# Delta rule stage: output gate blocks of the last token group moved into the four last steps, normalised rows reloaded in parts, the next stage's weights given other places

## The reference

```python
h = _rmsnorm(x, norm_w)
u = (h @ w_in).astype(f32)
gla_u, rwkv_u = u[..., :GLA_IN], u[..., GLA_IN:]
...
gla_out = o.reshape(B, T, GLA_VW) * jax.nn.silu(gg)
...
rg = rwkv_u[..., RWKV_SHIFT_W:]                      # output gate, the "z" blocks
mixed = shifted_cols + (prev - shifted_cols) * rwkv_mu
r, rk, rv, wl, al = _split(mixed, RWKV_SHIFT_SPLITS)
...
S = S * w_t + sa (kk_t a_t) + v_t k_t ;  y_t = S r_t   # per head, token after token
...
rwkv_out = (y + bonus) * jax.nn.silu(rg)
return x + jnp.concatenate([gla_out, rwkv_out], axis=-1) @ w_out
```

## Time and profile before

| | us |
|---|---|
| median of the runs (3) | 3676.9 |
| lowest and highest run | 3675.92, 3686.67 |
| span of the profiled execution | 3670.3 |

### The profile page before, as it was taken

How to read it: one execution, slowest core, us unless ns; L and a number is a source line. 1 busy time by engine, 2 the same in 40 slices (tenths; PEclk the granted TensorE clock), 3 DMA queues, 4 the chain that set the end, 5 groups by cost and what they waited for, 6 DMA issues and landing times. The chain is left out here.

```text
span 3670.3 us, 83152 instructions
## 1 busy us (share of the span) xinstructions
PE 3499.6 (95%) x34784; PEld 2817.1 (77%) x34784; DVE 2059.5 (56%) x4664; ACT 1718.7 (47%) x3161; POOL 1347.3 (37%) x1681
## 2 busy tenths in 40 slices
PE   8999998899899999999998989999999997999999
PEld 7878786688787877888786877777777776788777
DVE  4566766755655656555555436666666665344422
ACT  3455555522555556555553344444444442444522
POOL 5433331232445554545543323232232220544332
PEclk9999999999999999999998999999999998999999
DMA  4322211232110111101112341111111113322322
GB/s 136 90 66 81 61 53 35 81 104 93 30 41 24 41 30 30 41 24 41 30 33 89 129 144 48 43 43 39 46 38 43 43 37 111 82 74 70 104 81 92
DMA packets 252243, 231.26 MB, mean 63 GB/s; under 512 B 9120, under 2 KB 223072, under 8 KB 251872
## 3 DMA queue, kind: packets, MB, share of 16 engines
q1 hardware_dynamic: 251872, 225.94, 20.3%
HBM read 192.35 MB, written 33.55 MB: 62 GB/s over the span
## 5 line engine op out<-in xcount | busy, mean ns | idle before, releaser
L195 PE MATMUL bank<-hT_cut,arena_cut 128*128 128x512 f32 x2048 | 803.8, 393 | 0.0
L188 ACT ACTIVATE arena<-bank 128x512 f32<-128x512 f32 (+1 forms) x584 | 315.7, 569 | 578.4 <-PE bank L196 294.4
L194 PE MATMUL bank<-hT_cut,arena_cut 128*128 128x512 f32 x1240 | 553.9, 447 | 0.0
L196 PE MATMUL bank<-hT_cut,arena_cut 128*128 128x512 f32 x1240 | 488.6, 394 | 0.0
L194 PE MATMUL bank<-arena_cut,hT_cut 128*128 128x512 f32 (+1 forms) x1280 | 459.4, 359 | 28.5 <-DVE arena_cut L1148 23.9
L188 ACT ACTIVATE arena<-arena 128x512 f32<-128x512 f32 (+3 forms) x674 | 350.0, 555 | 251.9 <-POOL arena L1596 191.7
L195 PE MATMUL bank<-arena_cut,hT_cut 128*128 128x512 f32 (+1 forms) x1280 | 448.0, 350 | 0.0
L195 PEld LDWEIGHTS bank<-hT_cut,arena_cut 128*128 128x128 f32 x2048 | 387.4, 189 | 78.3 <-issue 18.3
L189 ACT ACTIVATE arena<-arena 128x256 f32<-128x256 f32 (+2 forms) x336 | 210.3, 627 | 417.2 <-DVE arena L178 192.7
L2846 POOL TENSOR_TENSOR arena_cut<-arena,arena_cut 128x256 fp32r<-128x256 f32 x272 | 218.1, 831 | 409.2 <-ACT arena_cut L188 409.1
L711 POOL TENSOR_TENSOR arena_cut<-arena,arena_cut 128x256 fp32r<-128x256 f32 x288 | 216.3, 778 | 410.8 <-ACT arena_cut L188 410.8
(11 more groups left out here) (269 smaller groups left out, 7192.2 us busy)
## 6 DMA issues: line engine op xcount, KB each, us to landing
arena<-in_w_in SPq DMA_DIRECT2D x100, 512.0 KB, 3.8
arena<-in_attn_w_in SPq DMA_DIRECT2D x144, 256.0 KB, 2.8
arena<-in_rec_w_in SPq DMA_DIRECT2D x62, 512.0 KB, 4.1
x_after<-arena SPq DMA_DIRECT2D x32, 512.0 KB, 2.6
arena<-x_after SPq DMA_DIRECT2D x32, 512.0 KB, 4.2
arena<-in_x SPq DMA_DIRECT2D x16, 512.0 KB, 3.6
h_after<-hT SPq DMA_DIRECT2D x4, 2048.0 KB, 7.7
hT<-h_after SPq DMA_DIRECT2D x4, 2048.0 KB, 16.8
```

Of the source, the lines that this page charges most:

```text
L188: return e.activation(out, a, f, bias=bias, scale=scale)
L194: pe.matmul(out, a[0], b[0], start=start, stop=False)
L195: pe.matmul(out, a[0], b[1], start=False, stop=False)
L196: return pe.matmul(out, a[1], b[0], start=False, stop=stop)
```

## The change

In `delta_rule`:
- The four z blocks of the last group (units 12 to 15) leave `front` and become a stream `gate(u)` of their own, one for each of steps 32 to 35, eight ticks each over the ten rounds. The odd steps of the last group have 11 ticks in place of 17, and `steps_in` and `bonus` come one and two ticks after the end of v.
- In the gate stream, at the end of each of those steps, ACT does `tanh`, DVE makes (tanh + 1) * z in `tz`, and `late(u)` multiplies it into `oT`. `carry` of the last group writes its output alone. Unit 15's `late` is the last operation of the stage on DVE.
- The hi part of group 3 is put into the columns of group 1 in place of group 0, and its rounding waits chunk by chunk for group 2's last z block.
- SP loads the columns of group 0 after the load of block v of unit 12, groups 1 and 3 after the last z block (now in step 35), and group 2 in `gla`, behind unit 1.
- Eight tiles of `front` are laid where `gla`'s value weights will be, and the three weight buffers stand first in both stages, so that `load_v(0)` waits for the last front instead of the last z block, and `load(0)` for the z block before the last. On SP's list both still stand behind the loads of groups 1 and 3.

In `gla`: the hi part of group 0 goes to the columns of group 2 of `hT`; ACT rounds group 0 as soon as its columns are loaded, ahead of `settle`, but behind `wide_split(0)`; group 2 is awaited by `lows(2)` and by its rounding.

```diff
-def gla(k):
-    freed = k.freed
+def gla(k, h_saved):
+    freed, ready, moved = k.freed, k.ready, k.moved
...
+    w_at = [k.room_cut(2 * KC * P) for _ in range(3)]
     wide = k.room_cut(4 * KC * P)
-    w_at = [k.room_cut(2 * KC * P) for _ in range(3)]
...
-    hi_of = lambda g, c: k.hT_cut[:, c, cols_of(g // 2 if g == 2 else 0)] if g else k.oT_cut[:, c // 2, T // 2 + c % 2 * G:T // 2 + (c % 2 + 1) * G]
+    hi_of = lambda g, c: k.hT_cut[:, c, cols_of((2, 0, 1, 0)[g])]
...
-        for done in freed:
+        for done in freed[0]:
             sp.wait_ge(*done)
         load_v(0)
+        for done in freed[1]:
+            sp.wait_ge(*done)
         load(0)
         k.settle(sp)
...
+            if u == 1:
+                sp.wait_ge(*Fpe.by("z1", 1))
+                sp.wait_ge(*moved[2])
+                sp.dma_start(k.hT[:, :, cols_of(2)], h_saved[:, :, cols_of(2)]).then_inc(*h_got.did("in"))
...
         wide_split(0)
+        for done in ready:
+            a.wait_ge(*done)
+        run(cut(0))
         split(0)
         k.settle(a)
-        run(cut(0))
         low_kept(0)
...
@@ in delta_rule @@
-    hi_of = lambda g, c: k.hT_cut[:, c, cols_of(g // 2 if g == 2 else 0)] if g else ...
+    hi_of = lambda g, c: k.hT_cut[:, c, cols_of(g // 2)] if g else ...
...
+              for p, kind in [(None, "w")] + [(p, kind) for p in range(4) for kind in ("krv" if g == LAST else "krvz")]]
+    blocks += [("z", LAST, p) for p in range(4)]
...
-            ahead, ticks, went = stream(front, 0), 17 + (8 if i % 8 == 0 else 0), 0
+            ahead, went = stream(front, 0) if i < SN else gate(UN - 4 + i - SN), 0
+            ticks = 8 if i >= SN else 11 if i >= SN - 8 and i % 2 else 17 + (8 if i % 8 == 0 else 0)
...
+            if n == index["v", LAST, 0]:
+                sp.wait_ge(*Zpe.by("z", 7))
+                load_h(0)
-        sp.wait_ge(*Fpe.by("z", UN - 1))
-        for g in range(NG):
-            sp.wait_ge(*moved[g])
-            sp.dma_start(k.hT[:, :, cols_of(g)], h_saved[:, :, cols_of(g)]).then_inc(*h_got[g].did("in"))
+        sp.wait_ge(*Zpe.by("z", UN - 1))
+        load_h(1)
+        load_h(3)
...
@@ on_pe, front @@
                 squares()
                 yield from block("v", g, p, Fpe)
-                yield from block("z", g, p, Fpe, {2: bonus})
-                yield
+                if g == LAST:
+                    yield
+                    yield
+                    bonus()
+                else:
+                    yield from block("z", g, p, Zpe, {2: bonus})
+                yield
+
+        def gate(u):
+            yield from block("z", *groups[u], Zpe)
...
@@ on_act @@
+        def gated(u):
+            a.wait_ge(*Zpe.by("z", u))
+            if u > UN - 4:
+                a.wait_ge(*Zm.by("m", u - UN + 3))
+            elif u:
+                a.wait_ge(*Zv.by("z", u - 1))
+            k.tanh(tz, fb.at("z", u), scale=0.5).then_inc(*Za.did("th"))
...
@@ on_dve, front @@
+                if g == LAST:
+                    yield
+                    steps_in()
+                    yield
+                    bonus()
...
+        def gate(u):
+            yield from block()
+            v.wait_ge(*Za.by("th", u))
+            stt(v, tz, tz, 1.0, fb.at("z", u), ALU.add, ALU.mult).then_inc(*Zv.did("z"))
+            if u < UN - 1:
+                late(u)
+
+        def late(u):
+            g, p = groups[u]
+            out = k.oT[:, 4 + p, cols_of(g)]
+            v.wait_ge(*Zv.by("z", u))
+            v.wait_ge(*Cv.by("out", 2 * u + 1))
+            v.tensor_tensor(out, out, tz, ALU.mult).then_inc(*Zm.did("m"))
...
+            if g == LAST:
+                ts(v, k.oT[:, 4 + p, tok], y_at, 0.5, ALU.mult).then_inc(*Cv.did("out"))
...
-        in_turn(nothing, solve, scores, carry, front)
+        in_turn(nothing, solve, scores, carry, front, gate)
+        late(UN - 1)
...
-    k.freed = [Fpe.by("z", UN - 1)]
+    k.freed = [[Fpe.by("bn", UN - 1), Fa.by("v2", UN - 1), Fv.by("bn", UN - 1), Fp.by("bk", UN - 1)], [Zpe.by("z", UN - 2)]]
+    k.ready = [h_got[0].by("in")]
+    k.moved = moved
```

More of the change, by code:

```diff
@@ L2325, in gla @@
     on_dve()
[L2326 to L2327 removed]
+    k.freed = [(3 + c, Fpe.by("v1", UN - 1)) for c in range(2)] + [
+        ((BN - 4 + i) % 3, Fpe.by(kinds[i], UN - 1)) for i in (1, 2, 3)]
     k.ready = [Fpe.by("z1", UN - 1), Bv.by("out1", 1)]
@@ L2351, in delta_rule @@
     w_lo, w_hi = ([x[1].rearrange("p (s c n) -> p s c n", s=2, c=KC)[:, s] for x in w_at] for s in range(2))
+    kf, r_at, gl, av, kat, b_at, sq, kk_at = (room(G) for _ in range(8))
     wa, up, cols = room(G), room(512), room(80)
@@ L2362, in delta_rule @@
     sh = room(G + 1)
-    kf, r_at, gl, av, kat, tz = (room(G) for _ in range(6))
+    tz = room(G)
     vf_at = rooms(2, G)
-    b_at, sq, kk_at, rk_at, tt, eb, en = (room(G) for _ in range(7))
+    rk_at, tt, eb, en = (room(G) for _ in range(4))
     ar_at, beta, kappa, bon_at = rooms(2, 2 * G), room(G), room(G), rooms(3, G)
@@ L2430, in taken, with in_turn @@
         return s.by(name, n)
-    def in_turn(cut, solve, scores, carry, front):
+    def in_turn(cut, solve, scores, carry, front, gate):
         rounds = 10
@@ L2789, in front @@
                 turn = p == 3 and g + 1 < NG
-                yield from block("z", g, p, {c: (lambda c=c: round_h(g + 1, c)) for c in range(KC)} if turn else {})
-                a.wait_ge(*Fpe.by("z", u))
-                k.tanh(tz, fb.at("z", u), scale=0.5).then_inc(*Fa.did("z"))
-                yield
+                if g == LAST:
+                    yield
+                    yield
+                else:
+                    yield from block("z", g, p, {c: (lambda c=c: round_h(g + 1, c)) for c in range(KC)} if turn else {})
+                    gated(u)
+                yield
+        def gated(u):
[6 more added lines that the diff above has]
+        def gate(u):
+            yield from block("z", *groups[u])
+            gated(u)
         def scores(s):
@@ L2881, in front, with gate @@
                 yield from block("v", g, p, {5: removal})
-                yield from block("z", g, p)
+                if g == LAST:
+                    yield
+                    yield
+                else:
+                    yield from block("z", g, p)
                 yield
+        def gate(u):
+            yield from block("z", *groups[u])
         split(0)
         k.settle(pool)
-        in_turn(nothing, nothing, nothing, nothing, front)
+        in_turn(nothing, nothing, nothing, nothing, front, gate)
     def on_dve():
@@ L2976, in front, with gate @@
                 mixed("v", vf_at[u % 2])
-                yield from block({1: steps_in, 5: bonus}, g + 1 if p == 3 and g + 1 < NG else None)
-                v.wait_ge(*Fa.by("z", u))
-                stt(v, k.oT[:, 4 + p, cols_of(g)], tz, 1.0, fb.at("z", u), ALU.add, ALU.mult).then_inc(*Fv.did("z"))
-                yield
+                if g == LAST:
+                    yield
+                    steps_in()
+                    yield
+                    bonus()
+                else:
+                    yield from block({1: steps_in, 5: bonus}, g + 1 if p == 3 and g + 1 < NG else None)
+                    v.wait_ge(*Za.by("th", u))
+                    stt(v, k.oT[:, 4 + p, cols_of(g)], tz, 1.0, fb.at("z", u), ALU.add, ALU.mult).then_inc(*Zv.did("z"))
+                yield
+        def gate(u):
+            yield from block()
+            v.wait_ge(*Za.by("th", u))
+            stt(v, tz, tz, 1.0, fb.at("z", u), ALU.add, ALU.mult).then_inc(*Zv.did("z"))
[7 more added lines that the diff above has]
+            v.tensor_tensor(out, out, tz, ALU.mult).then_inc(*Zm.did("m"))
         def halve(l, s, ring, steps, t1, vec):
```

34 lines of the change are left out of this document (23 added, 11 removed).

## The result

The changed kernel is slower: 3710.84 us (median of 4 runs, 3707.28 to 3714.4) against 3677.61 us for the kernel before in the same comparison. The ratio is 1.0084, 95% interval 1.0073 to 1.0096, so 27 to 35 us. The direction was the forecast one, the size was not: +33 in place of +14.5, above the range.

The account below looks back on a forecast made before the run. PE was taken as without gap while fronts run, with 22.7 us idle in steps 32 to 35. Terms -9.2 + 11.1 + 11.1 + 1.5 = +14.5 us on 3676.9 gave 3691 us, range 3671 to 3703.

Parts of the forecast that it names:

- Odd steps: The last group's four odd steps: 25.7 us each in place of 28.0, transposes waiting for DVE's `ka`; -9.2 us.
- Even steps: Steps 26, 28 and 30, between the last group's odd steps: no term in the sum, so 0.
- Late steps: Steps 32 to 35, to the stage's end: z chunks, the gate's chain and table loads cost +11.1 us net.
- the rival with PE at 1.2 GHz in the late steps: In steps 32 to 35 z costs twice its time in two of them: +12 more, 3703 us; chance 0.12.
- Loads: Groups 1 and 3 land late, first value products come 25.4 us after the last z product; net +11.1 us.
- a head start of DVE's rests: At GLA's start the value products run beside DVE's rests, now further ahead: 2.0 us given back.
- Small ones: Loads of group 0 beside unit 12 and group 2 in `gla` stall PE: +1.5 us; other changes nothing.
- PE stays the bound: Rival for the last group's odd steps: -22 in place of -9.2, sum +1.7, 3679 us; chance 0.20.
- the whole of z hidden: Rival: steps 32 to 35 take in all of z, -6.6, with odd steps -22; sum -16, 3661 us; chance 0.12.
- loads at the end cost nothing: Rival at the next stage's start: `settle` is met before the stage ends; sum +3.4, 3680 us; chance 0.08.

Follow-up runs that it names:

- v early: The changed kernel with 17 ticks kept in the last group's odd steps, z's ticks left empty: 3697.3 us, ratio to the kernel before 1.0049.
- the tanh table: The changed kernel with a one-column tanh added at the end of odd steps 25, 27 and 29: 3706.7 us, ratio to the kernel before 1.0071.
- the clock: The changed kernel with the last group's bonus product multiplied five times in place of once: 3705.3 us, ratio to the kernel before 1.0071.
- gate deferred: The changed kernel with DVE's two operations of a late gate moved behind the next step's fourth tick: 3698.7 us, ratio to the kernel before 1.0054.
- groups 1 and 3 behind the weights: The changed kernel with these groups loaded in GLA behind the first weights, only their users waiting: 3696.35 us, ratio to the kernel before 1.0045.
- reload alone: The changed kernel with the last group's z blocks back in the odd steps, all else kept: 3676.9 us, ratio to the kernel before 0.9995.

## Why the prediction was off

**Odd steps: right.** Forecast -9.2, measured -8.1. PE does wait for `ka` behind DVE's carry end, as the sum of DVE's rows had it, and "v early" takes the wait away. The missing 1.1 us are in steps 29 and 31, where the granted clock is 0.98 and 0.96.

**Even steps: the step that failed.** The prediction's sum has no term for steps 26, 28 and 30, and so put them at nothing without a reason. They cost +7.2 us. Two things reach into them from an odd step. The tanh of the moved gate also served the next step: before, it left the tanh table loaded ("ACT_TABLE_LOAD" at 3050.41, lies at an odd step's end); without it the load falls in the middle of the even step, ahead of the carry's square: 1.1 us each, taken away by "the tanh table". And behind the wait that I had rightly forecast PE starts the next step at the lower clock: 1.0 to 1.5 us each, taken away by "the clock". I had looked for the lower clock only in the late steps, as a rival. Together that is 7.2 of the 14.5 us missing; it ate most of the gain of the odd steps.

**Late steps: right in mechanism, somewhat too small.** +11.1 forecast, +13.2 measured in the profile after; each step is within 1.1 us. In four other profiles with the same late code it is 14.1 to 17.7 us, with the granted clock lower in step 32, 34 or 35. So the rival with PE at 1.2 GHz in the late steps, priced at +12, came in part, up to 4.5 us more than in the profile after, and why one execution gets it and another does not stays open. That the gate's tanh, with its table, holds DVE at the next step's start is shown by the waits and by "gate deferred". A change of table costs the load's 1.28 us alone, as the sum had it: in step 35 of the kernel after, ACT's copies end at 3123.13, the load starts 0.02 us behind them, and the tanh 0.01 us behind the load.

```profile
3123.15 1.28 ACT L188 ACT_TABLE_LOAD   x1
3124.44 0.60 ACT L188 ACTIVATE arena<-bank 128x512 f32<-128x512 f32 x1
```

**Loads: right to the first value product, wrong behind it.** 25.4 us from the last z product were forecast; the last z product starts at 3137.05 and is listed to 3137.44, so it is 25.2 to 25.5. The move behind the weights gives 12 of these back. But I subtracted 2.0 for a head start of DVE's rests. They start 2.6 us ahead of the first value product where it was 1.2, and take 2.6 us more than before, beside POOL. That is +3.8 of the missing.

**Small ones: near by luck.** I took 1.5 us for the loads of group 0 and group 2, from the stall beside the loads of step 32. Neither costs anything here. Step 24, with the load of group 0 beside it, takes 33.81 us after and 33.80 before; the unit of GLA beside the load of group 2 takes 43.1 us in both profiles. The +1.9 us lie in other units of GLA, and they are not the change's: "groups 1 and 3 behind the weights", "v early" and "the clock" have that load too and take the 298.6 us of before. The gain of spreading the loads is in steps 32 and 33 of "reload alone", 2.7 us, at the edge of what can be measured.

The rival "PE stays the bound" is out, as are "the whole of z hidden" and "loads at the end cost nothing". My range was too narrow on the slow side: its only slow rival was the clock in the late steps, and none stood for an unchanged step next to a changed one.

## What to carry to other kernels

Work that is moved out of a step takes with it what it did for the next one: here the function table that it left loaded, and the busy time without which TensorE began the next step below 2.4 GHz. When an edit lets an engine wait in one step, look for the price in the step behind it. And before moving the last reader of a buffer later, list what waits for that buffer's refill: here a stage's `settle` made everything wait for rows that are first read some 75 us later.

## What the runs showed of the hardware

Behind an idle time of 2.8 us in a stream of small products the granted clock of the next step was 0.94 in place of 1.00, 1.5 us of TensorE time in step 26; four repeated products ahead of the wait, 0.8 us each (busy time 25.31 in place of 21.95), held it at 1.00. The same code doesn't always get the same clock: step 34, with a wait of 3.0 us, had 1.00, 0.92 or 0.84, depending on the execution.

A VectorE subtraction of 128x512 takes 1.21 us beside a GpSimd subtraction and 0.68 alone, and a GpSimd one of 128x256 takes 1.18 in place of 0.73: eight of VectorE's took 8.1 us beside GpSimd's, and 5.4 nearly alone.
